# Two banks of a value row instead of one added by VectorE in a one-core decoder layer

## The chip, the cores and the metric

The kernel runs on one core of a Trainium2 chip. The metric is the device time of one execution in microseconds (us); the time before is the median of three runs.

## The reference, cut to what matters

The kernel computes one decoder layer in float32 for 256 tokens of width 2048. Its first part (projection, convolution, sparse attention, output projection, layer norm) isn't touched by the change. The second part is PEER, a layer of single-neuron experts: each token has 128 chosen experts (8 heads of 16) out of 16384, and the output is the sum of the experts' value rows, each times a weight.

```python
def block(i):
    ...
    ub = u_tab[eb]
    h = jax.nn.gelu(jnp.einsum('td,thed->the', xb, ub), approximate=False)
    vb = v_tab[eb]
    return jnp.einsum('the,thed->td', gb * h, vb)
...
y = peer(x, peer_wq[l], peer_sub_keys[l], peer_u[l], peer_v[l])
x = layer_norm(ALPHA * x + y, ln2_g[l], ln2_b[l])
```

`u_tab` and `v_tab` lie side by side in one table in HBM, `uv_tab`: an expert is one line of 2048 u values and 2048 v values.

## The kernel before, in words

**Rows.** A "row" s (0 to 255) is one of the 128 expert slots of one group of 128 tokens: each of the 128 partitions holds the line of that token's expert (`row[k]`, 128 x 4096: u in the first half, v in the second). Rows 0 to 127 belong to token group 0, rows 128 to 255 to group 1. There are seven places (`PLACE[s]`) for rows, used in turn, so a place takes row s+7 when row s is done with. Some popular keys are computed densely for all tokens (`dense_part`, `v_dense`); the gather of a token whose expert is dense is skipped by its index.

**Gathers.** GpSimd (POOL in the profile) issues each gather as an indirect DMA (L546). From row 166 on a row is fetched in two gathers, in the order u(s), v(s-1), u(s+1), v(s) and so on. The gather u(s) waits for the dot product of row s-7 (`dots_done`); v(s) waits in `place_read` for TensorE to be done with row s-7 (`y_done`) and, for the rows of `ADDED`, for VectorE's addition of it (`y_last_done`).

**What is done with a row.** VectorE (DVE) makes the dot product of u and x (`dot`, L1886, a multiply and sum over 128x2048, followed by a short read of the accumulator). ScalarE (ACT) applies GELU (L1312), makes the weight (L1324), and scales the value half in place by it (L1339), in two instructions. TensorE (PE) adds the scaled value half into the four PSUM banks of the token group by transposes against an identity (`add_turned`, L924), 128 columns each, so sixteen for all four banks; PSUM holds the sum with tokens and columns exchanged. The partitions of some rows are turned by halves or mirrored, which the identity undoes.

**The rows of `ADDED`.** These are rows `VALUES_AT` to `TOKEN_AT` - 1, which is 166 to 249, 84 rows. For these TensorE leaves out the last bank (columns 1536 to 2047), and VectorE adds weight times value for them into an SBUF sum (`add_last`, L1897): one sum, `y_last`, for the rows that aren't mirrored and one for the mirrored ones. In VectorE's program `add_last(s - 1)` stands right behind `dot(s)`. From row 166 to 239 TensorE also has the dense experts' value products between the rows (`v_dense`, L1042), 96 parts; their 24 dense blocks of 1 MB are loaded through SP's queue.

**The end.** From about row 241 group 0 is turned back and gets its layer norm on VectorE between the dots (L1959, L1963, L1968, L1977). After row 249 ScalarE copies the four banks of group 1 out (`back_copy`), in the order 2, 3, 0, 1, and TensorE transposes them back (`turn_back`, L948); into bank 3 it also adds the two SBUF sums by two matmuls (L957). The last six rows, 250 to 255, are added token by token: banks 0 and 1 by TensorE (L935, the first two of these rows three banks), the others by VectorE (`add_token`, L2075). `add_token(250)` stands in VectorE's program behind the dots of 251 to 253 and waits until banks 2 and 3 are turned back. Then comes the layer norm of group 1 and the output.

**Bookkeeping.** `scaled` counts ScalarE's scaling instructions, two for each row below 250. `dynamic_dma_scratch_size` is the part of SBUF, per partition, that is set aside for the descriptors of GpSimd's DMAs.

Of the kernel before, what the change touches and what calls it, by code (L numbers as in the profile page):

```python
# [15 lines left out]
P = 128  # L16
D = 2048
# [3 lines left out]
DC = D // 2  # L21
# [30 lines left out]
ALL = TI * SLOTS  # L52
WIDER_AT = 36
PLACE = [s % PLACES if s < WIDER_AT else (s - WIDER_AT + PLACES) % (PLACES + 1) for s in range(ALL)]
# [5 lines left out]
TOKEN_AT = ALL - TAIL  # L60
# [27 lines left out]
VALUES_AT = ROW2_AT + 4  # L88
# [25 lines left out]
ADDED = range(VALUES_AT, TOKEN_AT)  # L114
# [17 lines left out]

SPLIT_USES = [sum(in_two(r) and PLACE[r] == PLACE[s] for r in range(s + 1)) for s in range(ALL)]
SPLITS = ALL - SPLIT


def layer(nc, xT, x_tok, w_stream, w_kw, w_sub, conv_p, cln, bucket1h, rel_bias,
          b_out, ln1_col, ln_rows, uv_tab, dense_u, out):
    with ExitStack() as ctx:
        def sb(name, shape, dt=F32):  # L140
            return ctx.enter_context(nc.sbuf_tensor(name, shape, dt))
# [7 lines left out]
        def bank(i, n):  # L149

            return ps[4 * (1 - i) + n]
# [59 lines left out]

        scratch = sb("scratch", [P, 7680])
        x1_mirrored = sb("x1_mirrored", [P, D])
        at = {"attention": 0, "peer": 0}

        def tmp(half, cols):
# [88 lines left out]
        def at_early(name, shape, offset, dt=F32):  # L305
            return nc.alloc_sbuf_tensor_at(name, shape, dt, offset=early0 + offset)
# [12 lines left out]
        slot_key = [cand[0], cand[1], qc]  # L319
        back = [back_first[:, :], cand_both]  # L320
        key_of = [at_early(f"key_of{c}", [P, TI, SLOTS], 4096 + 1024 * c) for c in range(2)]
        y_last = [at_early("y_last", [P, 512], 4096), at_early("y_last_mirrored", [P, 512], 2048)]
        row_gate = at_early("row_gate", [P, TI, SLOTS], 6144)
        popular = at_early("popular", [P, PK], 7168)
        ones = at_early("ones", [P, PK], 7680)
# [3 lines left out]

        def scaled_by(s):  # L330

            return 2 * (s + 1) if s < TOKEN_AT else TOKEN_AT + s + 1

        def weight_of(s):

# [269 lines left out]
        def _(pe):  # L605
# [308 lines left out]
            def add_turned(s):  # L914

                i, k = ROW_OF[s][0], PLACE[s]
                if mirrored(s):
                    order = ident_both if split(s) else ident_mirrored
                else:
                    order = ident_turned if split(s) else ident  # L920
                for half in range(2):
                    pe.wait_ge(scaled, 2 * s + half + 1)
                    for b in range(8 * half, 12 if half and s in ADDED else 8 * half + 8):
                        last = pe.matmul(bank(i, b // 4)[:, b % 4 * P:(b % 4 + 1) * P], row[k][:, D + b * P:D + (b + 1) * P], order[:, :],  # L924
                                         is_transpose=True, start=False, stop=True, skip_group_check=True)
                last.then_inc(y_done, 1)
# [15 lines left out]
            def turn_back(i, banks):  # L942

                for q in banks:
                    n = BACK_ORDER[i][q]
                    pe.wait_ge(back_copied, 4 * i + q + 1)
                    for c in range(4):
                        last = pe.matmul(bank(i, n)[:, c * P:(c + 1) * P], back[q % 2][:, c * P:(c + 1) * P], ident[:, :],  # L948
                                         is_transpose=True, start=c == 0, stop=True, skip_group_check=True)
                    if i == 0:  # L950
                        for c in range(4):
                            last = pe.matmul(bank(0, n)[:, c * P:(c + 1) * P], x1[:, 0, (4 * n + c) * P:(4 * n + c + 1) * P], ident[:, :],
                                             is_transpose=True, start=False, stop=True, skip_group_check=True)
                    if i == 1 and n == 3:
                        pe.wait_ge(y_last_done, len(ADDED))
                        for y, order in zip(y_last, (ident_turned[:, :], ident_both)):
                            last = pe.matmul(bank(1, 3), order, y[:, :], start=False, stop=True, skip_group_check=True)  # L957
                    last.then_inc(back_turned, 1)

            def unit_part(u, part):  # L960
# [135 lines left out]
        def _(act):  # L1096
# [211 lines left out]
            def gelu(s):  # L1308

                i, j = ROW_OF[s]  # L1310
                act.wait_ge(dots_done, s + 1)
                act.activation(dots[:, s:s + 1], dots[:, s:s + 1], ACT.Gelu).then_inc(gelu_done, 1)  # L1312
                r = RANKED.index((i, j // TOP))
                if j % TOP == 0:
                    act.wait_ge(gates_done, r + 1 if r < 2 else r + 2)
                elif s == SPLIT:
                    act.wait_ge(gates_done, 3)
                act.wait_ge(gelu_done, s + 1)
                if split(s):
                    if s == SPLIT or j % TOP == 0:  # L1320
                        act.wait_ge(turn_ready, max(r, 1))
                    c = split_col(s)
                    for to, of in ((slice(HALF, P), slice(0, HALF)), (slice(0, HALF), slice(HALF, P))):
                        whole = act.activation(weight_turned[to, c:c + 1], dots[of, s:s + 1], ACT.Identity, scale=row_gate[of, i, j:j + 1])  # L1324
                else:
                    whole = act.activation(weight_of(s), dots[:, s:s + 1], ACT.Identity, scale=row_gate[:, i, j:j + 1])
                whole.then_inc(weight_done, 1)
                act.wait_ge(weight_done, s + 1)
                w = weight_turned[:, split_col(s):split_col(s) + 1] if split(s) else weight_of(s)
                if s >= TOKEN_AT:  # L1330
                    if BEFORE_IT[s] >= TOKEN_AT:
                        act.wait_ge(y_done, BEFORE_IT[s] + 1)
                    act.activation(diag[PLACE[s]], ident_turned[:, :] if split(s) else ident[:, :], ACT.Identity, scale=w).then_inc(scaled, 1)
                    return
                if split(s):
                    act.wait_ge(v_half_in[PLACE[s]], v_half_from[PLACE[s]] + 16 * SPLIT_USES[s])
                for half in range(2):
                    v = row[PLACE[s]][:, D + half * DC:D + (DC + 512 if half and s in ADDED else (half + 1) * DC)]
                    act.activation(v, v, ACT.Identity, scale=w).then_inc(scaled, 1)  # L1339

            def park(n):
# [87 lines left out]
        def _(dve):  # L1429
# [459 lines left out]
            def add_last(s):  # L1889

                k, n, c = PLACE[s], ADDED.index(s), split_col(s)
                y = y_last[mirrored(s)]
                dve.wait_ge(weight_done, s + 1)
                dve.wait_ge(v_half_in[k], v_half_from[k] + 16 * SPLIT_USES[s])
                if n:
                    dve.wait_ge(y_last_done, n)
                dve.scalar_tensor_tensor(out=y[:, :], in0=row[k][:, D + 3 * 512:2 * D], scalar=weight_turned[:, c:c + 1],  # L1897
                                         in1=y[:, :], op0=ALU.mult, op1=ALU.add).then_inc(y_last_done, 1)

            def turn_identity():  # L1900
# [269 lines left out]
```

## Time and profile before

| | |
|---|---|
| median of 3 runs | 1567.0 us (1566.94 to 1567.02) |
| the profiled execution's own time | 1572.39 us |
| its span, first to last instruction | 1570.6 us |
| busy: PE, DVE, ACT, POOL | 91%, 82%, 60%, 45% of the span |
| granted TensorE clock, mean | 0.973 of full speed |
| moved by DMA | 538.79 MB |
| rows 166 to 249 | from 1181 us to about 1539 us of the span (first and last addition) |

The span is what the trace shows; the profiled execution's own time is 1.8 us more, and the runs without the profiler are shorter than both. The busy shares are means over stages with different limits. PE is TensorE's matmuls, PEld its weight loads.

### The profile page before, as it was taken

The numbers are of one execution on the slowest core, as the hardware profiler recorded it, in microseconds if no ns is written. First come the engines' busy times: TensorE is split into PE (matmuls) and PEld (weight loads), VectorE is DVE, ScalarE is ACT, GpSimd is POOL, SyncE is SP. The second block draws the span as 40 slices with busy tenths as digits, with TensorE's granted clock in tenths as the row PEclk, the third lists the DMA queues.
The fourth block names the chain that finished last, engine by engine and source line by source line (L and its number), as shares of the span: only waits on it lengthen the run. The fifth ranks groups of instructions, "written<-read, shape, count | busy, mean of one in ns | idle before, by whom it ended". The sixth has DMA issues, their size and how long they took to land.

```text
span 1570.6 us, 26584 instructions
## 1 busy us (share of the span) xinstructions
PE 1427.8 (91%) x10100; PEld 1303.1 (83%) x10100; DVE 1293.9 (82%) x2290; ACT 947.3 (60%) x1578; POOL 712.7 (45%) x463
## 2 busy tenths in 40 slices
PE   9999999999999979999999898888899889879965
PEld 7999899988889868888888787877878879779962
DVE  5689999866796898998999898989977667657788
ACT  5433345553255557787878677677776556546673
POOL 0100111100021237766677555444468868647883
PEclk9999999999999989999999999999889999999988
DMA  7574543466499999999999999999999999999995
GB/s 263 175 244 177 194 178 140 154 268 245 170 419 425 426 421 390 417 417 416 398 400 417 400 355 386 394 380 421 409 390 364 418 416 413 418 415 396 415 369 212
DMA packets 85487, 538.79 MB, mean 343 GB/s; under 512 B 25898, under 2 KB 26570, under 8 KB 29642
## 3 DMA queue, kind: packets, MB, share of 16 engines
q0 software_dynamic: 63808, 399.96, 63.1%
q1 hardware_dynamic: 20884, 137.00, 22.8%
q8 instruction: 76, 1.25, 0.3%
q14 instruction: 47, 0.39, 0.1%
q10 hardware_dynamic: 672, 0.21, 0.1%
HBM read 682.45 MB, written 4.19 MB: 437 GB/s over the span
## 4 chain that ended last, share of the span: by engine, by line
DMA 35%; PE 35%; DVE 16%; issue 7%; ACT 5%; POOL 2%; SPq 0%; POOLq 0%; DVEq 0%; ACTq 0%
DMA uv_row<-in_uv_tab,turned 32%; DVE uv_row L1886 8%; PE psum L612 7%; PE psum L614 7%; PE psum L613 7%; PE psum L924 5%; PE psum L968 4%; ACT uv_row L1339 2%; POOL uv_row L546 2%; DMA uv_row<-in_uv_tab,eid 2%; DMA w_raw<-in_w_stream 1%; PE psum L858 1%; PE psum L1000 1%; PE psum L742 1%; DVE w_lo L1461 1%
## 5 line engine op out<-in xcount | busy, mean ns | idle before, releaser
L546 POOL DMA_INDIRECT uv_row<-in_uv_tab,turned x392 | 622.2, 1587 | 340.1 <-PE psum L924 198.5
L1339 ACT ACTIVATE uv_row<-uv_row,turned 128x1024 f32<-128x1024 f32 x452 | 459.2, 1063 | 176.6 <-DMA uv_row<-in_uv_tab,turned 160.7
L1886 DVE CUSTOM_DVE_ANT_0 uv_row<-uv_row,x 128x2048 f32<-128x2048 f32 x143 | 327.8, 2292 | 66.4 <-DMA uv_row<-in_uv_tab,turned 53.5
L1886 DVE CUSTOM_DVE_ANT_0 uv_row<-uv_row,x_mirrored 128x2048 f32<-128x2048 f32 x113 | 259.4, 2295 | 59.8 <-DMA uv_row<-in_uv_tab,turned 52.4
L612 PE MATMUL psum<-xT_hi,w_hi 128*128 128x256 f32 x640 | 183.8, 287 | 4.0 <-DVE w_lo L1461 3.5
L924 PE MATMUL psum<-popular,uv_row 128*128 128x128 f32 x1160 | 149.4, 281 | 40.2 <-ACT uv_row L1339 39.9
L1042 PE MATMUL psum<-scratch,dense_unit 128*128 128x128 f32 x1536 | 185.8, 277 | 0.0
L924 PE MATMUL psum<-scratch,uv_row 128*128 128x128 f32 x1160 | 148.2, 280 | 39.5 <-ACT uv_row L1339 39.2
L613 PE MATMUL psum<-xT_lo,w_hi 128*128 128x256 f32 x640 | 181.7, 284 | 0.0
L614 PE MATMUL psum<-xT_hi,w_lo 128*128 128x256 f32 x640 | 181.6, 284 | 0.0
L1042 PEld LDWEIGHTS psum<-scratch,dense_unit 128*128 128x128 f32 x1536 | 179.7, 194 | 0.0
L924 PEld LDWEIGHTS psum<-popular,uv_row 128*128 128x128 f32 x1160 | 132.3, 144 | 56.1 <-ACT uv_row L1339 52.9
L1000 PE MATMUL psum<-x1T,dense_unit 128*128 128x256 f32 x768 | 178.7, 379 | 0.0
L924 PEld LDWEIGHTS psum<-scratch,uv_row 128*128 128x128 f32 x1160 | 131.5, 144 | 53.8 <-ACT uv_row L1339 50.7
L1111 ACT ACTIVATE w_hi<-w_raw 128x2048 fp32r<-128x2048 f32 x62 | 118.8, 1916 | 85.9 <-DMA w_raw<-in_w_stream 85.9
L1461 DVE TENSOR_TENSOR w_lo<-w_raw,w_hi 128x2048 fp32r<-128x2048 f32 x62 | 141.7, 2287 | 28.9 <-ACT w_hi L1111 28.1
L1000 PEld LDWEIGHTS psum<-x1T,dense_unit 128*128 128x128 f32 x768 | 139.9, 190 | 15.8
L924 PE MATMUL psum<-ident,uv_row 128*128 128x128 f32 x864 | 114.8, 286 | 20.1 <-ACT uv_row L1339 19.8
L612 PEld LDWEIGHTS psum<-xT_hi,w_hi 128*128 128x128 f32 x640 | 123.4, 193 | 8.0 <-issue 3.5
L924 PEld LDWEIGHTS psum<-ident,uv_row 128*128 128x128 f32 x864 | 101.3, 148 | 30.2 <-ACT uv_row L1339 27.6
L613 PEld LDWEIGHTS psum<-xT_lo,w_hi 128*128 128x128 f32 x640 | 123.4, 193 | 0.1
L614 PEld LDWEIGHTS psum<-xT_hi,w_lo 128*128 128x128 f32 x640 | 123.4, 193 | 0.0
(306 smaller groups left out, 2108.0 us busy)
## 6 DMA issues: line engine op xcount, KB each, us to landing
w_raw<-in_w_stream SPq DMA_DIRECT2D x63, 1024.0 KB, 4.8
dense_unit<-in_dense_u SPq DMA_DIRECT2D x24, 1024.0 KB
dense_unit<-in_uv_tab SPq DMA_DIRECT2D x24, 1024.0 KB
wq_first<-in_w_stream SPq DMA_DIRECT2D x8, 1024.0 KB
uv_row<-in_uv_tab,turned POOLq DMA_INDIRECT x392
wq_third<-in_w_stream SPq DMA_DIRECT2D x4, 1024.0 KB
xT_raw<-in_xT SPq DMA_DIRECT2D x4, 512.0 KB, 5.4
turned_rows<-dist_row POOLq DMA_DIRECT2D x1, 2048.0 KB
```

The lines of the kernel that those rows point to most:

```text
L546: pool.indirect_dma_start(dst, None, tab, bass.IndirectOffsetOnAxis(ap=ids, axis=0), bounds_check=tab.shape[0] - 1, oob_is_err=False).then ...
L612: pe.matmul(dst, a[0], b[0], start=first, stop=False)
L613: pe.matmul(dst, a[0], b[1], start=False, stop=False)
L614: return pe.matmul(dst, a[1], b[0], start=False, stop=last)
L924: last = pe.matmul(bank(i, b // 4)[:, b % 4 * P:(b % 4 + 1) * P], row[k][:, D + b * P:D + (b + 1) * P], order[:, :], is_transpose=True, st ...
L968: last = pe.matmul(ps[0][:, 0:S], w[:, c, :], x1T[:, c, :], start=c == 0, stop=c == KC - 1)
L1000: last = pe.matmul(side[v % 2][:, 0:S], w[:, c, :], x1T[:, c, :], start=c == 0, stop=c == KC - 1)
L1042: last = pe.matmul(bank(i, n)[:, b % 4 * P:(b % 4 + 1) * P], dense_unit[v % 2][:, b * P:(b + 1) * P], mixed[:, v, i * P:(i + 1) * P], star ...
L1111: act.activation(w_hi[k], w_raw[k], ACT.Copy).then_inc(hi_done, 1)
L1339: act.activation(v, v, ACT.Identity, scale=w).then_inc(scaled, 1)
L1461: dve.tensor_tensor(w_lo[k], w_raw[k], w_hi[k].bitcast(F32), ALU.subtract).then_inc(lo_dve, 1)
L1886: dve.tensor_tensor_reduce(row[k][:, 0:D], row[k][:, 0:D], x_row, 1.0, 0.0, ALU.mult, ALU.add, dots[:, s:s + 1]).then_inc(dots_done, 1)
```

## The change

For rows 166 to 249 VectorE's sum takes columns 1024 to 2047 of the value half, two banks, where it took 1536 to 2047. TensorE transposes eight blocks of a row (banks 0 and 1) where it did twelve. ScalarE scales the first 1024 columns in one instruction, where it did 1024 and then 512. `y_last` and `y_last_mirrored` are twice as wide; `turn_back` adds them into banks 2 and 3, with two matmuls each, so the wait for all 84 additions now stands ahead of bank 2, the first one. `SCALED` counts ScalarE's instructions before a row. To make room for the wider sum, the descriptors' part of SBUF is halved, from 8192 to 4096 bytes of a partition.

```diff
--- before.py
+++ after.py
@@ -132,6 +132,7 @@
 
 SPLIT_USES = [sum(in_two(r) and PLACE[r] == PLACE[s] for r in range(s + 1)) for s in range(ALL)]
 SPLITS = ALL - SPLIT
+SCALED = [sum(2 if r < VALUES_AT else 1 for r in range(s)) for s in range(ALL + 1)]
 
 
 def layer(nc, xT, x_tok, w_stream, w_kw, w_sub, conv_p, cln, bucket1h, rel_bias,
@@ -211,6 +212,7 @@
 
         scratch = sb("scratch", [P, 7680])
         x1_mirrored = sb("x1_mirrored", [P, D])
+        y_last_mirrored = sb("y_last_mirrored", [P, 1024])
         at = {"attention": 0, "peer": 0}
 
         def tmp(half, cols):
@@ -319,7 +321,7 @@
         slot_key = [cand[0], cand[1], qc]
         back = [back_first[:, :], cand_both]
         key_of = [at_early(f"key_of{c}", [P, TI, SLOTS], 4096 + 1024 * c) for c in range(2)]
-        y_last = [at_early("y_last", [P, 512], 4096), at_early("y_last_mirrored", [P, 512], 2048)]
+        y_last = [at_early("y_last", [P, 1024], 2048), y_last_mirrored]
         row_gate = at_early("row_gate", [P, TI, SLOTS], 6144)
         popular = at_early("popular", [P, PK], 7168)
         ones = at_early("ones", [P, PK], 7680)
@@ -329,7 +331,7 @@
 
         def scaled_by(s):
 
-            return 2 * (s + 1) if s < TOKEN_AT else TOKEN_AT + s + 1
+            return SCALED[s + 1]
 
         def weight_of(s):
 
@@ -918,9 +920,9 @@
                     order = ident_both if split(s) else ident_mirrored
                 else:
                     order = ident_turned if split(s) else ident
-                for half in range(2):
-                    pe.wait_ge(scaled, 2 * s + half + 1)
-                    for b in range(8 * half, 12 if half and s in ADDED else 8 * half + 8):
+                for half in range(1 if s in ADDED else 2):
+                    pe.wait_ge(scaled, SCALED[s] + half + 1)
+                    for b in () if half and s in ADDED else range(8 * half, 8 * half + 8):
                         last = pe.matmul(bank(i, b // 4)[:, b % 4 * P:(b % 4 + 1) * P], row[k][:, D + b * P:D + (b + 1) * P], order[:, :],
                                          is_transpose=True, start=False, stop=True, skip_group_check=True)
                 last.then_inc(y_done, 1)
@@ -951,10 +953,10 @@
                         for c in range(4):
                             last = pe.matmul(bank(0, n)[:, c * P:(c + 1) * P], x1[:, 0, (4 * n + c) * P:(4 * n + c + 1) * P], ident[:, :],
                                              is_transpose=True, start=False, stop=True, skip_group_check=True)
-                    if i == 1 and n == 3:
+                    if i == 1 and n >= 2:
                         pe.wait_ge(y_last_done, len(ADDED))
                         for y, order in zip(y_last, (ident_turned[:, :], ident_both)):
-                            last = pe.matmul(bank(1, 3), order, y[:, :], start=False, stop=True, skip_group_check=True)
+                            last = pe.matmul(bank(1, n), order, y[:, (n - 2) * 512:(n - 1) * 512], start=False, stop=True, skip_group_check=True)
                     last.then_inc(back_turned, 1)
 
             def unit_part(u, part):
@@ -1334,8 +1336,8 @@
                     return
                 if split(s):
                     act.wait_ge(v_half_in[PLACE[s]], v_half_from[PLACE[s]] + 16 * SPLIT_USES[s])
-                for half in range(2):
-                    v = row[PLACE[s]][:, D + half * DC:D + (DC + 512 if half and s in ADDED else (half + 1) * DC)]
+                for half in range(1 if s in ADDED else 2):
+                    v = row[PLACE[s]][:, D + half * DC:D + (half + 1) * DC]
                     act.activation(v, v, ACT.Identity, scale=w).then_inc(scaled, 1)
 
             def park(n):
@@ -1894,7 +1896,7 @@
                 dve.wait_ge(v_half_in[k], v_half_from[k] + 16 * SPLIT_USES[s])
                 if n:
                     dve.wait_ge(y_last_done, n)
-                dve.scalar_tensor_tensor(out=y[:, :], in0=row[k][:, D + 3 * 512:2 * D], scalar=weight_turned[:, c:c + 1],
+                dve.scalar_tensor_tensor(out=y[:, :], in0=row[k][:, D + DC:2 * D], scalar=weight_turned[:, c:c + 1],
                                          in1=y[:, :], op0=ALU.mult, op1=ALU.add).then_inc(y_last_done, 1)
 
             def turn_identity():
@@ -2157,7 +2159,7 @@
     }
     ins["dense_u"] = np.asarray(peer_u)[0].reshape(PK, PK, KC, P).transpose(0, 3, 2, 1).reshape(PK, P, UNIT)
     nc = _bacc.Bacc("TRN2", target_bir_lowering=False, num_devices=1,
-                    dynamic_dma_scratch_size=8192)
+                    dynamic_dma_scratch_size=4096)
     arrays, args = {}, {}
     for name, a in ins.items():
         a = np.ascontiguousarray(a)
```

## Rows read from the trace of the kernel before

**Rows 1.** The page: busy time by engine; then the chain that ended last, by engine.

```profile
PE 1427.8 (91%) x10100; PEld 1303.1 (83%) x10100; DVE 1293.9 (82%) x2290; ACT 947.3 (60%) x1578; POOL 712.7 (45%) x463
...
DMA 35%; PE 35%; DVE 16%; issue 7%; ACT 5%; POOL 2%; SPq 0%; POOLq 0%; DVEq 0%; ACTq 0%
```

**Rows 2.** Windows: busy us and count of each engine, granted clock, DMA share, GB/s.

```profile
1182.00:1200.00 18.00, 18.00 (x150) 16.59 (x149) 16.78 (x18) 15.39 (x32) 16.17 (x7) 1.00 0.87 308
1200.00:1410.00 210.00, 180.31 (x1545) 175.00 (x1544) 136.37 (x136) 110.32 (x227) 150.60 (x102) 0.98 1.02 416
1410.00:1460.00 50.00, 44.89 (x397) 44.09 (x398) 37.25 (x39) 31.71 (x65) 35.31 (x22) 1.00 1.00 398
1500.00:1550.00 50.00, 34.16 (x202) 27.34 (x201) 47.40 (x54) 35.31 (x73) 41.12 (x21) 0.86 0.96 365
```

**Rows 3.** Groups on ACT, 1200 to 1500 us: busy, mean ns, idle before.

```profile
L1339 ACT ACTIVATE uv_row<-uv_row,turned 128x1024 f32<-128x1024 f32 x68 | 78.1, 1149 | 130.0 <-DMA uv_row<-in_uv_tab,turned 124.0 <-issue 5.4 <-ACT turned L1324 0.4
L1339 ACT ACTIVATE uv_row<-uv_row,turned 128x512 f32<-128x512 f32 x68 | 48.1, 708 | 0.0
```

**Rows 4.** Groups on DVE, 900 to 1571 us.

```profile
L1938 DVE TENSOR_TENSOR first_key<-scratch 128x1024 f32<-128x1024 f32 x32 | 39.1, 1221 | 5.0 <-ACT qc L1376 5.0
L1897 DVE SCALAR_TENSOR_TENSOR y_last<-uv_row,turned,y_last 128x512 f32<-128x512 f32 x42 | 31.5, 751 | 13.2 <-issue 13.2
```

**Rows 5.** The page: costliest groups, same columns.

```profile
L1461 DVE TENSOR_TENSOR w_lo<-w_raw,w_hi 128x2048 fp32r<-128x2048 f32 x62 | 141.7, 2287 | 28.9 <-ACT w_hi L1111 28.1
```

**Rows 6.** Timeline, 1300 to 1316 us: start, us, instructions, idle before.

```profile
1304.48 1.47 PE L924 MATMUL psum<-scratch,uv_row 128*128 128x128 f32 x12
```

**Rows 7.** Timeline of DVE, 1460 to 1571 us.

```profile
1506.13 2.29 DVE L1886 CUSTOM_DVE_ANT_0 uv_row<-uv_row,x_mirrored 128x2048 f32<-128x2048 f32 x1 [1.05 <-DMA uv_row<-in_uv_tab,turned]
...
1510.56 0.70 DVE L1959 BATCH_NORM_STATS2 stats<-psum 128x6 f32<-128x512 f32 x1 [0.48 <-PE psum L952]
...
1513.51 0.75 DVE L1897 SCALAR_TENSOR_TENSOR y_last_mirrored<-uv_row,turned,y_last_mirrored 128x512 f32<-128x512 f32 x1
...
1538.52 0.75 DVE L1897 SCALAR_TENSOR_TENSOR y_last_mirrored<-uv_row,turned,y_last_mirrored 128x512 f32<-128x512 f32 x1
...
1558.08 2.90 DVE L1959 BATCH_NORM_STATS2 stats<-psum 128x6 f32<-128x512 f32 x4
```

**Rows 8.** Timeline of PE, 1530 to 1560 us.

```profile
1541.12 1.02 PE L957 MATMUL psum<-y_last,popular 128*128 128x512 f32 x2
...
1544.24 12.18 PE L935 MATMUL psum<-uv_row,scratch 128*128 128x512 f32 x28
```

**Rows 9.** Timeline of POOL, 1172 to 1203 us.

```profile
1181.39 3.11 POOL L546 DMA_INDIRECT uv_row<-in_uv_tab,turned  x1 [0.30 <-issue]
1184.81 2.57 POOL L546 DMA_INDIRECT uv_row<-in_uv_tab,turned  x1 [0.30 <-issue]
1187.68 2.57 POOL L546 DMA_INDIRECT uv_row<-in_uv_tab,turned  x1 [0.30 <-issue]
...
1199.48 0.99 POOL L546 DMA_INDIRECT uv_row<-in_uv_tab,turned  x1 [0.30 <-issue]
```

**Rows 10.** Timeline of DVE, 1172 to 1203 us.

```profile
1180.83 0.48 DVE L1995 MEMSET y_last_mirrored<- 128x512 f32 x1
1181.35 2.29 DVE L1886 CUSTOM_DVE_ANT_0 uv_row<-uv_row,x_mirrored 128x2048 f32<-128x2048 f32 x1
...
1184.23 2.28 DVE L1886 CUSTOM_DVE_ANT_0 uv_row<-uv_row,x 128x2048 f32<-128x2048 f32 x1
...
1187.11 2.28 DVE L1886 CUSTOM_DVE_ANT_0 uv_row<-uv_row,x_mirrored 128x2048 f32<-128x2048 f32 x1
```

**Rows 11.** Timeline of DVE, 790 to 800 us.

```profile
795.25 2.37 DVE L1886 CUSTOM_DVE_ANT_0 uv_row<-uv_row,x 128x2048 f32<-128x2048 f32 x1
```

**Rows 12.** Timeline of POOL, 790 to 800 us.

```profile
795.29 0.99 POOL L546 DMA_INDIRECT uv_row<-in_uv_tab,turned  x1 [0.30 <-issue]
```

## The prediction

> **What bounds the kernel now.** I read the page first: PE is busy for 91% and DVE for 82% of the span, and the chain is 35% DMA and 35% PE [rows 1]. Such means hide stages, so I cut the part that the change touches into windows [rows 2]. From 1200 to 1460 us the DMA share is 1.00 to 1.02 at 398 to 416 GB/s: the transfers are the bound there, and PE at 180.3 of 210 us and DVE at 136.4 of 210 have room. ACT scales 68 rows in 300 us [rows 3], so a row comes every 4.41 us. Two windows differ. From 1182 to 1200 us DMA falls to 0.87 and 308 GB/s, with PE, DVE and POOL all near full. From 1500 to 1550 us DVE is busy 47.4 of 50 us: VectorE bounds the end. The change has to be priced in three stages.
>
> **Part 1: what each engine gains or loses per row.** A 512-column addition takes 0.751 us and a 1024-column two-input operation 1.221 [rows 4], a 2048-column one 2.287 [rows 5]: 1.04 ns a column. So the wider addition takes 0.751 + 512 x 0.00104 = 1.28 us, 0.53 more, for 84 rows 45 us of DVE (low bound 1.22 us, as the row of 1024 columns, 0.47 more). ACT spent 1.149 + 0.708 us a row on scaling [rows 3] and keeps the first: 0.71 less. PE's twelve transposes take 1.47 us [rows 6], eight by proportion 0.98: 0.49 less, 41 us in all. If PE were the bound that would be the gain; but the DMA engines are full from 1200 us on, so neither PE's nor ACT's gain is worth anything there. DVE doesn't become the bound in the mean either: 210 us hold 48 rows, 136.4 + 48 x 0.53 = 162 us. A place is free 0.7 + 0.5 us sooner by TensorE and 0.5 later by VectorE, against a round of 7 x 4.41 = 31 us, which only changes how long a transfer queues. I take 0 from 1200 to 1500 us.
>
> **Part 2: the end.** DVE last waits at 1506.13 for a transfer (1.05 us) and at 1510.56 for PE (0.48 us) [rows 7]; from there its work is gapless. Before this, each longer addition is absorbed at the next wait for a transfer. In the stretch there are seven additions, from 1513.51 to 1538.52 [rows 7]: 7 x 0.53 = 3.7 us. The wait at 1510.56 covers most of the one before it, and PE arrives there sooner; I take 0.4 off: +3.3 us. Bounds: 2.9, and 5.3 if ten additions count. The wait for all 84 additions is moved ahead of bank 2 in `turn_back`. Behind it on PE stand the matmuls of two banks (one bank's two pairs take 1.7 us from 1541.12 on [rows 8]), two more banks, then L935; on ACT a copy. I work out that PE begins L935 about 5.4 us after the last addition, against 1544.24 - 1539.27 = 5.0 before. L935 takes 12.18 us [rows 8] and ends at 1556.4, while DVE reads its banks only in the third of the statistics that begin at 1558.08 [rows 7], near 1559.5: 3.1 us of cover, 2.7 after. `add_token(250)` stands 7 us behind the last addition, and its banks are ready after 4.5. So the moved wait costs 0; without its cover 0.4 us directly.
>
> **Part 3: the start, 1182 to 1200 us.** Here the addition acts through POOL. Each row needs two gathers. A gather that starts clear of DVE takes 0.99 us; in this stretch each takes 2.57, with 0.30 between, one for every dot [rows 9]. Laid beside DVE: the dot runs from 1184.23 for 2.28 us, the gather ends at 1187.38, 0.87 after it; the next starts at 1187.68, when the next dot has run since 1187.11, and waits for its end too [rows 9, 10]. So POOL issues one gather, half a row, per 2.88 us, and DMA runs dry.
>
> Will the longer addition let a second gather in between? The gather starts 1187.68 - 1184.23 = 3.45 us after the previous dot did. The next dot now starts 2.88 + 0.53 = 3.41 us after it, so the gather comes 0.04 to 0.05 us too late. The trace brackets what is too late: begun 0.04 us after a dot, at 795.29 against 795.25, a gather still took 0.99 us and the dot 0.08 more [rows 11, 12]; begun at 1181.39 against 1181.35, nearly the same lag, it took 3.11 us [rows 9, 10]. It is a knife's edge. The lag in the stretch works out at 0.045 to 0.047 us from unrounded starts, that of the second case was 0.046, that of the first 0.041, so I take it that the gathers keep waiting, now one per 3.41 us. While DVE has rows in hand the stage is paced by this. Six gathers wait, from 1181.39 on. I laid out the new sequence: the memsets are 0.53 us longer each (0.48 before [rows 10]), which lets the gather of 1181.39 in at once, 2.1 us sooner; then each of the following loses 0.53 us on the old schedule, and since DVE works off its rows more slowly, the pattern lasts some three dots longer than to 1199.48. The fourth gather after that stands 3.3 us later than before. Since DMA is the bound from there on, this lateness runs through to the end. I take +3.1 us. Bounds: +5 if the pattern lasts longer, and if every second gather does slip in (two per 3.41 us, 1.70 each), the whole dip comes back: (416 - 308) / 416 x 18 = 4.7 us [rows 2], of which I would count 4.0.
>
> The Trainium skill (SBUF — State Buffer, Who interferes with whom) says that a DVE instruction with two SBUF inputs contends with a GpSimd instruction that reads SBUF, and that the second one blocks fully until the first finishes; this trace agrees, with 2.57 us instead of 0.99. Going by that sentence alone, without the starting lags, more DVE time only means more blocking, which has the sign of my sum, +3.1.
>
> **The halved descriptor space.** No row shows a gather waiting for room. With seven places at most 14 gathers are under way; if only half of them fitted, that would still be 3.5 rows, 15 us of transfers at 4.41 us a row, so I cost it at 0.
>
> **Sum.** Against the profiled execution: span 1570.6 + 3.1 (start) + 0 (middle) + 3.3 (end) = 1577.0. Its own time lies 1.8 us above its span and the median of the runs 3.6 below the span; I apply the difference to the median: 1567.0 + 6.4 = 1573.4 us. The measurement tells 0.2% from no change, 3.1 us: slower, by 0.4%.
>
> **The rivals.**
> - *The second gather slips in (not slower).* The edge falls the other way: -4.0 at the start, -0.5 of the 2.2 us that the same formula gives for the dips of 1410 to 1460 us ((416 - 398) / 416 x 50 [rows 2]), +3.3 at the end: 1567.0 - 1.2 = 1565.8. It decides from 0.005 us of lag less, for instance if the addition takes 1.29 us, or if some jitter repeats in each dot. Against it: the lag as worked out lies on the waiting side. For it: the margin is smaller than I can know the addition.
> - *All dips go (faster).* As before, with the whole 4.7 + 2.2 back and 2.9 at the end: 1563.0.
> - *Only the end counts (a little slower).* Some gathers slip in, some wait, and the start comes out even; or PE, full for all 18 us [rows 2], holds the stretch and its 0.49 us a row pays for the rest: 1567.0 + 3.3 = 1570.3.
> - *TensorE's clock (much slower).* PE ran at 0.86 granted clock from 1500 to 1550 us, 34.2 of 50 us busy [rows 2], and now has less to do. If L935's 12.18 us fell to the lower level (1.2 instead of 2.4 GHz), 24.4 us, less 2.7 of cover, that is +9.5 on top of the forecast: 1582.9. It decides once PE is 2.7 us late. Against it: L935 is dense work and ran at full clock after a slack stretch.
> - *The descriptor space bites (slower).* Gathers clear of DVE would take over 0.99 us. At the start's rate for all of a second such stretch, another 4.7 us: 1578.1.
>
> **How the numbers follow.** Forecast 0.45, second gather slips in 0.19, all dips go 0.06, only the end 0.22, clock 0.04, descriptors 0.04. The forecast's own range is 1571.4 (+1.5, +2.9) to 1577.3 (+5.0, +5.3). Over 1570.1 lie the forecast, clock, descriptors and half of the end-only case: slower 0.64. Under 1563.9 lie the all-dips case and the edge of the second: faster 0.09. The same: 0.27. The range for 8 in 10 reaches from the middle of the case of the second gather to the forecast's upper part: 1565.3 to 1577.0.
>
> **What would show each step.** Right: L1897 at 1.28 us; one L1339 a row; eight transposes in 0.98 us; in the start stretch gathers of about 3.1 us, one per dot, dots 3.41 us apart, DMA below 308 GB/s and low for longer, then full to 1500 us; DVE gapless for some 60 us at the end, with seven or eight additions in it; L957 for two banks, ended before `add_token(250)`. Wrong: in the start stretch gathers that alternate between about 2.1 and 1.0 us, two per dot, and DMA near 416 GB/s (the second rival); a POOL that waits for `y_last` or PE while DMA is low; DVE gapless well before 1500 us, which puts more additions on the path; a wait of DVE for L935; gathers above 0.99 us with DVE idle.

## The result and the profile after

The changed kernel takes 1574.5 us (median of 7 runs, 1570.5 to 1576.5), the kernel before 1568.0 in runs beside it. The ratio is 1.0035, 95% interval 1.0019 to 1.0051, which on 1568 us is 5.5 us slower (3.0 to 8.0). In a later comparison it was 1.0046 (1.0032 to 1.0059). The forecast was 6.4 us slower.

The profiled execution of the changed kernel was its shortest (1570.5 us, span 1568.7), that of before a long one (1572.4), so the spans can't be compared. I had read the 1572.4 us as if profiling had made the run longer, but they lie within that kernel's scatter: its later runs took 1563.8 to 1575.7. The two traces differ by about 4 us already at row 0's dot, before the change has touched anything but the descriptor space and the places of the sums, and by 7.3 at row 166's, which starts at 1170.65 against 1177.93. From row 0's dot to row 166's, ahead of the first row that is treated differently, the changed kernel's two traces take 1.4 to 3.3 us less than that of the kernel before and that of `half_space` (the kernel before with the halved descriptor space, below); no run explains that. I therefore measure from inside the stage: from the start of row 166's dot to that of row 243's, and from there to the end. The page's busy times, to be read against [rows 1]:

```profile
PE 1403.0 (89%) x9768; PEld 1274.8 (81%) x9768; DVE 1338.4 (85%) x2290; ACT 896.6 (57%) x1494; POOL 721.7 (46%) x463
...
PE 30%; DMA 30%; DVE 25%; ACT 6%; issue 6%; POOL 2%; SPq 0%; DVEq 0%; POOLq 0%; ACTq 0%
```

DVE has 44.5 us more (1338.4 against 1293.9), as 84 additions of 0.53 us should give, and PE 24.8 less, where 41 was forecast. Part of that gap is in the dense value products: 1536 of their matmuls took 193.1 us (L1044), 185.8 before, and PE was granted less clock in several of the windows below. The windows, to be read against [rows 2]; the columns are busy us and count of PE, PEld, DVE, ACT and POOL, the granted clock, DMA share and GB/s:

```profile
1182.00:1200.00 18.00, 14.98 (x132) 14.60 (x131) 17.24 (x17) 9.47 (x20) 16.17 (x7) 0.99 0.91 322
1200.00:1410.00 210.00, 163.85 (x1327) 157.78 (x1326) 161.62 (x138) 83.88 (x183) 164.96 (x102) 0.94 1.01 414
1410.00:1460.00 50.00, 43.50 (x376) 41.82 (x375) 43.84 (x37) 23.43 (x51) 38.89 (x23) 1.00 1.01 405
1460.00:1500.00 40.00, 32.53 (x260) 31.54 (x259) 35.77 (x33) 19.09 (x42) 34.74 (x18) 0.91 0.97 373
1500.00:1550.00 50.00, 32.16 (x140) 23.42 (x141) 49.05 (x50) 26.35 (x58) 29.13 (x21) 0.66 0.87 348
```

DMA is still starved at 1182 to 1200 us (322 GB/s, 308 before), and now also at 1460 to 1500 (373, 413 before). The first window says little about the change, though: the stage begins 7.3 us earlier in this trace, so the same 18 us hold other rows, and `half_space` has 328 GB/s there without any of the wider additions. DVE is busy 49.05 of 50 us in the last window. PE's clock is at 0.66 there, 0.86 before and 0.76 in `half_space`. The groups of the addition and the scaling, with mean ns, against [rows 3, 4]:

```profile
L1899 DVE SCALAR_TENSOR_TENSOR y_last<-uv_row,turned,y_last 128x1024 f32<-128x1024 f32 x42 | 53.8, 1281 | 8.8 <-issue 8.7
```

```profile
L1341 ACT ACTIVATE uv_row<-uv_row,turned 128x1024 f32<-128x1024 f32 x69 | 79.3, 1149 | 166.5 <-DMA uv_row<-in_uv_tab,turned 151.9 <-issue 13.9 <-ACT turned L1326 0.7
```

The addition takes 1.281 us (1.28 forecast), and ACT scales once per row. PE's eight transposes, in the timeline against [rows 6], take 1.04 us, 0.98 forecast:

```profile
1180.78 1.04 PE L926 MATMUL psum<-scratch,uv_row 128*128 128x128 f32 x8
```

The heart of it is the first burst. POOL's timeline, against [rows 9]:

```profile
1178.59 3.10 POOL L548 DMA_INDIRECT uv_row<-in_uv_tab,turned  x1 [0.30 <-issue]
1182.00 3.10 POOL L548 DMA_INDIRECT uv_row<-in_uv_tab,turned  x1 [0.30 <-PE psum L926]
1185.40 3.11 POOL L548 DMA_INDIRECT uv_row<-in_uv_tab,turned  x1 [0.30 <-issue]
1188.82 3.10 POOL L548 DMA_INDIRECT uv_row<-in_uv_tab,turned  x1 [0.30 <-issue]
1192.22 3.10 POOL L548 DMA_INDIRECT uv_row<-in_uv_tab,turned  x1 [0.30 <-PE psum L926]
1195.63 0.99 POOL L548 DMA_INDIRECT uv_row<-in_uv_tab,turned  x1 [0.30 <-issue]
1196.93 2.22 POOL L548 DMA_INDIRECT uv_row<-in_uv_tab,turned  x1 [0.31 <-issue]
```

and DVE's in the same stretch, against [rows 10]:

```profile
1178.55 2.28 DVE L1888 CUSTOM_DVE_ANT_0 uv_row<-uv_row,x 128x2048 f32<-128x2048 f32 x1
...
1180.76 1.28 DVE L1899 SCALAR_TENSOR_TENSOR y_last_mirrored<-uv_row,turned,y_last_mirrored 128x1024 f32<-128x1024 f32 x1
1181.95 2.28 DVE L1888 CUSTOM_DVE_ANT_0 uv_row<-uv_row,x_mirrored 128x2048 f32<-128x2048 f32 x1
...
1185.36 2.28 DVE L1888 CUSTOM_DVE_ANT_0 uv_row<-uv_row,x 128x2048 f32<-128x2048 f32 x1
...
1188.77 2.28 DVE L1888 CUSTOM_DVE_ANT_0 uv_row<-uv_row,x_mirrored 128x2048 f32<-128x2048 f32 x1
...
1192.18 2.28 DVE L1888 CUSTOM_DVE_ANT_0 uv_row<-uv_row,x 128x2048 f32<-128x2048 f32 x1
...
1195.99 2.29 DVE L1888 CUSTOM_DVE_ANT_0 uv_row<-uv_row,x_mirrored 128x2048 f32<-128x2048 f32 x1 [0.33 <-DMA uv_row<-in_uv_tab,turned]
```

Read a line of the one beside a line of the other: gather 1185.40, dot 1185.36; gather 1188.82, dot 1188.77; gather 1192.22, dot 1192.18. Every gather comes 0.04 to 0.05 us after the dot, waits for its end and takes 3.10 us. The dots are 3.41 us apart. Only when a dot comes late, at 1195.99 after 0.33 us of waiting for a transfer, does the gather of 1195.63 find no dot running, and it takes 0.99 us. In the second execution of the changed kernel (`after_again` below) the same pattern holds in this burst, with one gather that slips through, and goes on to row 175's dot instead of row 172's.

At the end DVE last waits for a transfer at 1500.51; the addition behind that dot and the statistics follow, and the last of the 84 additions begins at 1535.86, against [rows 7]:

```profile
1500.51 2.29 DVE L1888 CUSTOM_DVE_ANT_0 uv_row<-uv_row,x_mirrored 128x2048 f32<-128x2048 f32 x1 [0.25 <-DMA uv_row<-in_uv_tab,turned]
...
1502.73 1.29 DVE L1899 SCALAR_TENSOR_TENSOR y_last<-uv_row,turned,y_last 128x1024 f32<-128x1024 f32 x1
1503.93 1.43 DVE L1961 BATCH_NORM_STATS2 stats<-psum 128x6 f32<-128x512 f32 x2
...
1535.86 1.27 DVE L1899 SCALAR_TENSOR_TENSOR y_last_mirrored<-uv_row,turned,y_last_mirrored 128x1024 f32<-128x1024 f32 x1
...
1556.17 2.90 DVE L1961 BATCH_NORM_STATS2 stats<-psum 128x6 f32<-128x512 f32 x4
```

From that dot (row 243) to the end of the span it is 68.2 us; before, from 1506.13, it was 64.5, and 65.6 in `half_space`. The waits of 0.29 and 0.48 us for PE ahead of the first two statistics, which the trace before has behind its dot of 1506.13, are gone. PE's timeline there, against [rows 8]:

```profile
1538.38 1.92 PE L959 MATMUL psum<-y_last,popular 128*128 128x512 f32 x2
1540.08 1.44 PE L959 MATMUL psum<-y_last_mirrored,scratch 128*128 128x512 f32 x2
...
1541.80 1.02 PE L959 MATMUL psum<-y_last,popular 128*128 128x512 f32 x2
1542.66 1.02 PE L959 MATMUL psum<-y_last_mirrored,scratch 128*128 128x512 f32 x2
...
1544.92 12.18 PE L937 MATMUL psum<-uv_row,scratch 128*128 128x512 f32 x28
```

`turn_back` now has four pairs (the first two at the lower clock). L937 starts at 1544.92 and ends at 1557.1, DVE needs the first of its banks at about 1557.6, in the third of the statistics that start at 1556.17: it never waits, but the cover has shrunk to 0.5 us.

### The profile page after: what moved, and what is told of

Its sections match the earlier page's. It is cut to its first block, busy times and chain, and to the rows that moved or that the text cites. A ratio compares the mean times of both kernels' runs of the same rounds, so it can differ in the third digit from the quotient of the medians.

```text
span 1568.7 us, 25836 instructions
## 1 busy us (share of the span) xinstructions
PE 1403.0 (89%) x9768; PEld 1274.8 (81%) x9768; DVE 1338.4 (85%) x2290; ACT 896.6 (57%) x1494; POOL 721.7 (46%) x463
## 4 chain that ended last, share of the span: by engine, by line
PE 30%; DMA 30%; DVE 25%; ACT 6%; issue 6%; POOL 2%; SPq 0%; DVEq 0%; POOLq 0%; ACTq 0%
DMA uv_row<-in_uv_tab,turned 27%; DVE uv_row L1888 8%; PE psum L926 7%; DVE scratch L1535 4%; PE psum L614 4%; PE psum L616 4%; PE psum L615 4%; DVE w_lo L1463 4%; PE psum L970 4%; ACT uv_row L1341 3%; DMA uv_row<-in_uv_tab,eid 2%; PE psum L1002 2%; POOL uv_row L548 2%; DMA w_raw<-in_w_stream 1%; PE psum L1044 1%
## 5 line engine op out<-in xcount | busy, mean ns | idle before, releaser
L548 POOL DMA_INDIRECT uv_row<-in_uv_tab,turned x392 | 641.1, 1635 | 323.5 <-PE psum L926 168.8
L1341 ACT ACTIVATE uv_row<-uv_row,turned 128x1024 f32<-128x1024 f32 x368 | 407.6, 1144 | 208.7 <-DMA uv_row<-in_uv_tab,turned 189.5
L1044 PE MATMUL psum<-scratch,dense_unit 128*128 128x128 f32 x1536 | 193.1, 283 | 0.8 <-DMA dense_unit<-in_uv_tab 0.6
L1044 PEld LDWEIGHTS psum<-scratch,dense_unit 128*128 128x128 f32 x1536 | 187.0, 200 | 1.2 <-DMA dense_unit<-in_uv_tab 0.8
L926 PE MATMUL psum<-popular,uv_row 128*128 128x128 f32 x992 | 132.6, 284 | 61.8 <-ACT uv_row L1341 61.0
L926 PEld LDWEIGHTS psum<-popular,uv_row 128*128 128x128 f32 x992 | 114.7, 146 | 78.0 <-ACT uv_row L1341 74.1
L926 PE MATMUL psum<-scratch,uv_row 128*128 128x128 f32 x992 | 132.6, 284 | 44.4 <-ACT uv_row L1341 44.2
L926 PEld LDWEIGHTS psum<-scratch,uv_row 128*128 128x128 f32 x992 | 115.0, 146 | 60.0 <-ACT uv_row L1341 57.0
```

Of the source, the lines that this page charges most:

```text
L548: pool.indirect_dma_start(dst, None, tab, bass.IndirectOffsetOnAxis(ap=ids, axis=0), bounds_check=tab.shape[0] - 1, oob_is_err=False).then ...
L1044: last = pe.matmul(bank(i, n)[:, b % 4 * P:(b % 4 + 1) * P], dense_unit[v % 2][:, b * P:(b + 1) * P], mixed[:, v, i * P:(i + 1) * P], star ...
```

## The experiments

All are timed beside the kernel before, ratios over at least eight runs but for the repeat of the changed kernel (six); 0.001 is 1.6 us. Three sets were timed at different times, each beside its own runs of the kernel before (medians 1568.9, 1567.9 and 1569.2 us), so ratios are compared and not times.

**Which part of the stage, and the descriptor space.** First the kernel before with the descriptor space alone halved:

```diff
-                    dynamic_dma_scratch_size=8192)
+                    dynamic_dma_scratch_size=4096)
```

> The kernel before with the descriptor space of 4096 bytes alone. My account (start and end of the stage on VectorE) expects no change, 0 within 1 us. If the halved descriptor space is what costs, all of the change's 5.5 to 6.5 us appear here, with gathers above 0.99 us where VectorE is idle.

Ratio 0.9996 (0.9983 to 1.0009). The descriptor space costs nothing that the runs can tell (-2.7 to +1.4 us).

Then the change for one part of the rows each. `WIDE` are the rows with two banks on VectorE, the others of `ADDED` are done as before:

```diff
+WIDE = range(VALUES_AT, 238)        # the other kernel: range(238, TOKEN_AT)
+SCALED = [sum(1 if r in WIDE or r >= TOKEN_AT else 2 for r in range(s)) for s in range(ALL + 1)]
...
-                for half in range(1 if s in ADDED else 2):
+                for half in range(1 if s in WIDE else 2):
...
+                of = slice(0 if s in WIDE else 512, 1024)
+                dve.scalar_tensor_tensor(out=y[:, of], in0=row[k][:, D + DC + of.start:2 * D], ...
```

> The changed kernel with two banks on VectorE only for rows 166 to 237; rows 238 to 249 go back to one bank, twelve transposes and two scalings. My account expects the end's 3.3 us to be gone and the start's 3.1 to stay: +2 to +4 us against the kernel before. If only the end counts: 0. If VectorE's load costs evenly over all rows: 72/84 of the whole, +5 us.

> The opposite: two banks on VectorE only for rows 238 to 249, one bank for rows 166 to 237. My account expects the end's +3.3 us (3 to 5) and nothing at the start but the longer memsets. If only the start counts: 0. If VectorE's load costs evenly over all rows: 12/84 of the whole, +1 us.

> The changed kernel unaltered, as the reference of this call: +5.5 us (3 to 8) against the kernel before by the ratio already measured; by my account about the sum of the two partial kernels, whose costs lie at opposite ends of the stage.

Early 1.0040 (1.0025 to 1.0056), +6.3 us; late 1.0022 (1.0009 to 1.0034), +3.4; the whole 1.0046 (1.0032 to 1.0059), +7.2. The late part costs what I expected, the early one more: its +6.3 us (3.9 to 8.8) is nearer to the +5 of a cost spread evenly over all rows than to my +2 to +4, and only the experiments with a wait, below, decide between the two. Their sum, 9.7 us, is above the 5.5 and 7.2 us of the whole, though the intervals don't exclude that they add up. From the traces, starts of dots of the rows named and the end of the span, in us:

```
                  166 to 172   166 to 190   166 to 243   243 to end
before               18.1        104.2        328.2        64.5
half_space           19.5        104.1        327.9        65.6
after                21.5        104.6        329.9        68.2
after_again          22.7        105.5        330.0        68.7
wide_early           21.5        105.0        330.6        71.4
wide_late            18.9        102.9        326.8        68.8
dve_alone            21.5        108.7        337.8        70.3
pe_act_alone         19.4        100.8        325.9        63.9
nudge_all            22.1        101.5        327.3        70.1
nudge_early          23.1        101.3        324.4        65.6
nudge_early_2        22.1        101.5        324.6        64.3
nudge_few            22.1         99.5        322.7        70.1
nudge_230            22.2        101.5        324.4        65.7
wait_in_before       18.4        104.8        328.8        65.3
```

Each line is one execution, and two of the same kernel differ by up to 1.3 us. Without a wait, the first burst is 3.4 to 4.7 us longer than before wherever VectorE adds two banks in it, but in the two executions of the changed kernel only 0.4 and 1.2 us of that are left at row 190, and 1.7 and 1.8 at row 243. The first column shows VectorE's own pace and not what the gathers lose: the kernels with the wait have 22.1 to 23.1 us in it and are ahead of before at row 190. The early kernel has 6.9 us more than before in its last column although its last rows are as before. Its DVE timeline shows why:

```profile
1533.97 2.31 DVE L1889 CUSTOM_DVE_ANT_0 uv_row<-uv_row,x 128x2048 f32<-128x2048 f32 x1 [0.52 <-DMA uv_row<-in_uv_tab,last_id]
...
1539.70 2.29 DVE L1889 CUSTOM_DVE_ANT_0 uv_row<-uv_row,x 128x2048 f32<-128x2048 f32 x1 [2.28 <-DMA uv_row<-in_uv_tab,last_id]
...
1543.28 2.29 DVE L1889 CUSTOM_DVE_ANT_0 uv_row<-uv_row,x 128x2048 f32<-128x2048 f32 x1 [1.28 <-DMA uv_row<-in_uv_tab,last_id]
...
1546.99 2.29 DVE L1889 CUSTOM_DVE_ANT_0 uv_row<-uv_row,x 128x2048 f32<-128x2048 f32 x1 [1.41 <-DMA uv_row<-in_uv_tab,last_id]
...
1550.81 2.29 DVE L1889 CUSTOM_DVE_ANT_0 uv_row<-uv_row,x 128x2048 f32<-128x2048 f32 x1 [0.85 <-DMA uv_row<-in_uv_tab,last_id]
...
1554.84 2.29 DVE L1889 CUSTOM_DVE_ANT_0 uv_row<-uv_row,x 128x2048 f32<-128x2048 f32 x1 [1.06 <-DMA uv_row<-in_uv_tab,last_id]
```

The last rows' gathers land late, and DVE waits for the last six of them in turn, 7.4 us in all; before, it waited for none of them. POOL comes late out of the middle: when row 243's dot starts it has 22 gathers still to start, against 18 before and 20 and 22 in the two executions of the changed kernel. Between these dots and that of row 249 the one-bank rows of the early kernel come 4.2 to 4.6 us apart and POOL starts two gathers per dot; with two banks they come 4.8 to 5.2 us apart and it starts three. At row 249's dot the early kernel still has 10 gathers to start, the kernel before 5, and the changed kernel, whose backlog was nearly as large, 2 and 4. So in this trace the faster tail doesn't give POOL the time to catch up. It is one execution, 2.5 us above its kernel's median.

**VectorE's part and TensorE's part alone.**

```diff
 # dve_alone: the kernel before, but each addition over 1024 columns
+                y2 = y[:, :].rearrange("p (o n) -> p o n", o=2)
+                twice = row[k][:, D + 3 * 512:2 * D].rearrange("p (o n) -> p o n", o=1).to_broadcast([P, 2, 512])
+                dve.scalar_tensor_tensor(out=y2, in0=twice, ..., in1=y2, ...)
 # pe_act_alone: the changed kernel, but VectorE adds bank 3 alone
+                dve.scalar_tensor_tensor(out=y[:, 512:], in0=row[k][:, D + 3 * 512:2 * D], ..., in1=y[:, 512:], ...)
```

> VectorE's cost alone: PE's twelve transposes and ACT's two scalings stay, VectorE's addition works on 1024 columns by taking columns 1536 to 2047 twice into a sum of two banks, of which one is used. If PE's and ACT's relief is worth nothing, this costs what the whole change costs, +5 to +7 us; if their relief pays for part of it, more, +9 us and up.

> PE's and ACT's relief alone: eight transposes and one scaling of 1024 columns a row, VectorE adds one bank as before, and bank 2 of the value rows 166 to 249 is left out of the result. My account: nothing to gain while DMA and VectorE set the time, 0 to -1.5 us. If PE is the bound of the stage: -5 us or more.

VectorE's part alone costs 1.0041 (1.0019 to 1.0062), +6.4 us, TensorE's and ScalarE's relief alone gives nothing, 1.0012 (0.9999 to 1.0025), if anything 1.9 us more where I expected 0 to -1.5, though bank 2 of these rows is left out of the result and its work is done by no engine. By the timed runs PE is not the bound. The traces are less sure: the windows of `dve_alone`,

```profile
1182.00:1200.00 18.00, 17.79 (x162) 17.60 (x160) 16.88 (x15) 10.93 (x22) 16.25 (x6) 1.00 0.85 287
...
1410.00:1460.00 50.00, 47.09 (x407) 46.50 (x406) 44.85 (x39) 30.85 (x63) 39.28 (x21) 0.97 0.99 393
1460.00:1500.00 40.00, 36.88 (x320) 36.55 (x319) 33.67 (x30) 23.37 (x50) 35.43 (x16) 0.96 0.87 311
```

have PE at 47.1 of 50 us and DMA at 311 GB/s from 1460 to 1500, so with VectorE slower PE's relief may pay for some of it in that execution (337.8 us from row 166 to 243, against 330 with the relief). But it was the slowest of its kernel, 5.3 us above the median, and that of `pe_act_alone`, 2.3 us ahead of before at row 243, was the fastest of its own, 5.8 below. By the timed runs the difference between the two, 6.4 and 5.5 to 7.2 us, can't be told.

**The second gather.** This is the test of the 0.04 us. VectorE is made to wait for the end of its addition before the next dot starts:

```diff
                 dve.scalar_tensor_tensor(...).then_inc(y_last_done, 1)
+                if s in ADDED:                  # nudge_early: if s in WIDE, rows 166 to 237
+                    dve.wait_ge(y_last_done, n + 1)
```

> The changed kernel, in which VectorE waits for each addition's end before it starts the next dot. That puts the dot some 0.1 to 0.15 us later, so a gather that came 0.04 us too late should now slip in ahead of it. The account by the second gather expects the 3.1 us gathers to vanish between 1182 us and the end, the transfers to lose 5 to 8 us less from row 160 on, and the tail to pay about 7 x 0.15 = 1 us: 4 to 7 us faster than the changed kernel, so -2 to +3 us against the kernel before. If it is VectorE's load that costs, adding 84 x 0.15 us to it makes the time longer still: +8 us or more against before.

> Two banks on VectorE for rows 166 to 237 with that wait, one bank and no wait for rows 238 to 249. The account by the second gather expects the start and middle repaid and the tail as before: -2 to -5 us against the kernel before. If PE or ACT or the load of VectorE set the start and middle: as the kernel with two banks in rows 166 to 237, +6 us.

The wait adds DVE time to every row that has it, and the kernel gets faster than without it. With it everywhere the ratio is 1.0023 (1.0010 to 1.0037), +3.6 us against before: some 2 to 4 us less than the changed kernel, where I expected 4 to 7 less and at most +3 against before. With it in the early rows, and one bank in the late ones, 0.9985 (0.9972 to 0.9998), -2.4 us: 8.6 us below the same kernel without the wait. POOL's timeline in the burst of that kernel,

```profile
1189.86 0.99 POOL L549 DMA_INDIRECT uv_row<-in_uv_tab,turned  x1 [0.30 <-issue]
1191.15 1.93 POOL L549 DMA_INDIRECT uv_row<-in_uv_tab,turned  x1 [0.30 <-issue]
1193.39 0.99 POOL L549 DMA_INDIRECT uv_row<-in_uv_tab,turned  x1 [0.30 <-issue]
1194.69 1.93 POOL L549 DMA_INDIRECT uv_row<-in_uv_tab,turned  x1 [0.30 <-issue]
1196.92 0.99 POOL L549 DMA_INDIRECT uv_row<-in_uv_tab,turned  x1 [0.30 <-issue]
```

and DVE's,

```profile
1189.93 2.29 DVE L1889 CUSTOM_DVE_ANT_0 uv_row<-uv_row,x 128x2048 f32<-128x2048 f32 x1
...
1192.14 1.28 DVE L1901 SCALAR_TENSOR_TENSOR y_last_mirrored<-uv_row,turned,y_last_mirrored 128x1024 f32<-128x1024 f32 x1
1193.46 2.29 DVE L1889 CUSTOM_DVE_ANT_0 uv_row<-uv_row,x_mirrored 128x2048 f32<-128x2048 f32 x1
...
1195.68 1.28 DVE L1901 SCALAR_TENSOR_TENSOR y_last<-uv_row,turned,y_last 128x1024 f32<-128x1024 f32 x1
1196.99 2.29 DVE L1889 CUSTOM_DVE_ANT_0 uv_row<-uv_row,x 128x2048 f32<-128x2048 f32 x1
```

The dots are 3.53 us apart, 0.12 more than without the wait, and the gathers that came 0.04 us late now come 0.07 us early (1189.86 for 1189.93, 1193.39 for 1193.46) and take 0.99 us, and a second one follows under the dot. The windows say what it does for the transfers; the first line is the early kernel without the wait, the second that with it:

```profile
1182.00:1200.00 18.00, 17.59 (x159) 17.40 (x157) 16.45 (x15) 8.98 (x20) 16.17 (x7) 1.00 0.86 304
1182.00:1200.00 18.00, 18.00 (x152) 16.76 (x151) 17.02 (x15) 11.30 (x25) 15.26 (x10) 1.00 0.99 388
```

388 GB/s instead of 304; the two stages begin within 0.5 us of each other. From row 166's dot to row 190's it is 410 against 390 (before 397, the changed kernel 395 and 386). Counted over rows 166 to 249, the gathers of 3.05 us and more are 4 before, 23 and 29 in the two executions of the changed kernel, 27 in the early kernel, 1 and 0 in the two with the wait.

Is it the lag, or does such a wait help by itself? The same wait in the kernel before:

```diff
                                          in1=y[:, :], op0=ALU.mult, op1=ALU.add).then_inc(y_last_done, 1)
+                dve.wait_ge(y_last_done, n + 1)
```

> The kernel before with the same wait behind each addition of one bank. The account by the starting lag: the dot comes 0.13 us later but the gather is 0.58 us late there, so it goes on waiting and nothing is gained; seven waits of 0.13 in the tail cost 0.9 us: 0 to +2 us. If the wait helps in itself, whatever the lag: -2 to -5 us, as in the kernel with two banks.

Ratio 0.9995 (0.9982 to 1.0008): no gain. POOL's and DVE's timelines:

```profile
1185.34 2.69 POOL L546 DMA_INDIRECT uv_row<-in_uv_tab,turned  x1 [0.30 <-issue]
1188.34 2.69 POOL L546 DMA_INDIRECT uv_row<-in_uv_tab,turned  x1 [0.30 <-issue]
```

```profile
1184.88 2.29 DVE L1886 CUSTOM_DVE_ANT_0 uv_row<-uv_row,x_mirrored 128x2048 f32<-128x2048 f32 x1
...
1187.88 2.29 DVE L1886 CUSTOM_DVE_ANT_0 uv_row<-uv_row,x 128x2048 f32<-128x2048 f32 x1
```

The gather comes 0.46 us after the dot (1185.34 for 1184.88), and waits as ever. The wait helps only where it carries the dot past the gather.

**How far to go.** Three more with two banks and the wait in the first rows only:

```diff
+WIDE = range(VALUES_AT, 181)        # nudge_230: 230; nudge_early_2: 238, as nudge_early
```

> Two banks and the wait only for rows 166 to 180, one bank and no wait for the rest. If the first burst holds most of what the second gather can give, this repays the dip of 4 to 5 us without the middle's load on VectorE: -3 to -5 us against the kernel before. If the gain needs all rows up to 237, about -1 us.

> Two banks and the wait for rows 166 to 229. As the version to row 237, -2.4 us, or a little better, -3 us, if VectorE is already behind at row 230; worse if the last burst needs the second gather.

> The kernel with two banks and the wait for rows 166 to 237 once more, to narrow its interval: -2.4 us, between -4 and 0.

To row 180: 0.9981 (0.9967 to 0.9995), -3.0 us. To row 229: 0.9995 (0.9980 to 1.0010). To row 237 again: 0.9973 (0.9960 to 0.9987), -4.2 us, just beyond what I expected. The first burst alone holds as much as can be told from the runs; its trace is 5.5 us ahead of before at row 243 and loses that in the tail, where it waits for gathers again. The version to row 229 should lie with the others by its trace and does not by its runs; its profiled execution was 5.0 us below its median, the intervals overlap, and I leave that open. The version to row 237 beats both kernels in two separate comparisons.

## Why the prediction was right, and where it wasn't

**Part 1 (per row)** held: 1.281 us for the addition against 1.28, 1.04 against 0.98 for the transposes, one scaling. That PE's and ACT's relief is worth nothing by itself is what `pe_act_alone` shows, within 2 us. "I take 0 from 1200 to 1500 us" did not hold in the traces: DMA falls to 373 GB/s from 1460 to 1500 us.

**Part 2 (the end), +3.3 us.** Right in place and mechanism, perhaps a little small. From row 243's dot to the end it is +3.7 and +4.2 us in two executions (1.1 us less against `half_space`), and the late kernel costs +3.4 (1.4 to 5.3) by the timed runs. The gapless stretch begins one addition earlier than I counted: eight times 0.53 is 4.2, less the 0.77 us of waits for PE, 3.5. The moved wait cost nothing, as forecast, but its cover fell to 0.5 us instead of 2.7: L937 began 7.8 us after the last addition where I had worked out 5.4, with PE at the lower clock for the last transposes and the first two pairs. The clock rival was nearer than its chance of 0.04 suggests. The lower clock isn't the change's alone, though: with the descriptor space halved and nothing else, the two pairs took 1.91 and 1.88 us.

**Part 3 (the start), +3.1 us.** The mechanism was right to the hundredth of a microsecond: gathers 0.04 to 0.05 us too late, 3.10 us each, one per 3.41 us. What failed is the step "this lateness runs through to the end". Row 172 came 3.4 and 4.7 us late in the two executions, but at row 190 only 0.4 and 1.2 us were left. "The pattern lasts some three dots longer" held in one execution, which goes on to row 175's dot, and not in the other, which ends at row 172's as before. In place of the lateness that runs through, the runs show the same pattern again in later bursts, 23 and 29 gathers in all, and 1.7 and 1.8 us at row 243. So start and middle together cost 2 us in the traces where I had 3.1 and 0, and the end 4 where I had 3.3; the sum came out right partly because the two errors have opposite signs. The partial kernels don't split the cost that way: the early one costs +6.3 us by itself. Two smaller things: "DMA below 308 GB/s" didn't show, it was 322, and the +1.5 us at the low end of this part's range had no working.

**The rivals.** The second gather that slips in was one delay of 0.12 us away, and I had priced it too well. Its case is `nudge_all`, two banks everywhere and the gathers let in: I had worked out 1.2 us less than before, and it took 3.6 more (1.6 to 5.8). In its trace start and middle gain 0.9 us, not 4.5, and the end costs 5.6, not 3.3; some 1.0 us of the end is eight waits of 0.12. That `nudge_early` came to 1565.2 us where I had 1565.8 is fortunate, since it has one bank in the tail. Only the end: +3.4 us is what the late kernel costs, and the changed kernel's 5.5 and 7.2 lie above it, with intervals that overlap. The descriptor space: nothing that can be told. What made `wide_early` cost more in the tail, POOL's backlog carried into it, I had not thought of. It is read from one trace, not tested apart.

## What to carry to other kernels

Where one engine issues the gathers and is shut out while another computes, look at when the gather starts within the other's period, not at the sum of busy times: a fraction of a microsecond decides between one and two gathers a period. A short wait on the computing engine can then make the kernel faster (8.6 us here), and work moved to it can cost in a stage that the transfers bound. An addition moved to the engine that bounds the end should stop some rows before the end, once the gathers keep up: with the wait that gained 6 to 8 us (0.9985 and 0.9973 against 1.0023), without it nothing that can be told (1.0040 against 1.0035 and 1.0046).

## What the runs showed of the hardware

A gather begun up to 0.044 us after a dot's start could still take 0.99 us, and the dot was then up to 0.08 us longer; one begun from 0.035 us on could already take 3.10 us. In the two executions of the changed kernel both occur between 0.035 and 0.044 us after the start; below that all pass, and from 0.045 us on all wait. What decides between the two within that gap, no run shows. The gather's end lies 0.86 to 0.88 us behind the end of the operation that shut it out. I had not expected so sharp an edge, nor that a kernel's dots and gathers, coupled by it, lock into a fixed lag of 0.04 us for five rows in a row.
